# Second block's inner norms by token tile: pooling projection and the up projections' first two chunks begin with tile 0

## What is computed

```python
def second_block(x, ...):
    for layer in range(DEPTH):                       # DEPTH = 2
        j = layer // 2
        if layer % 2 == 0:
            y = even_mixer(x, ...)                   # mLSTM beside forgetting attention
        else:
            y = odd_mixer(x, ...)                    # state-space heads beside a pooling branch
        x = layer_norm(ALPHA * x + y, ln1_g[layer], ln1_b[layer])
        f = conv_ffn(x, ffn_w_up[layer], ffn_conv_w[layer], ffn_conv_b[layer], ffn_w_down[layer])
        x = layer_norm(ALPHA * x + f, ln2_g[layer], ln2_b[layer])
    return x
```

## Time and profile before

| | us |
|---|---|
| median of 3 runs | 1237.4 (1235.99 to 1239.66) |
| the profiled execution | 1235.73 |
| its span | 1233.9 |
| TensorE's products busy | 1188.3 (96%) |
| TensorE's weight loads busy | 1063.8 (86%) |
| POOL busy | 940.8 (76%) |
| ACT busy | 676.7 (55%) |
| DVE busy | 586.9 (48%) |
| mean granted TensorE clock | 0.987 |

### The profile page before, as it was taken

One profiled execution on the slowest core, in us unless ns is written; L12 is line 12 of the kernel. 1 busy time (PEld: TensorE's weight loads), 2 busy tenths in 40 slices (PEclk: granted clock), 3 DMA queues, 4 the chain that ended last, 5 costly groups with the idle time before them and its releaser, 6 DMA issues.

```text
span 1233.9 us, 20217 instructions
## 1 busy us (share of the span) xinstructions
PE 1188.3 (96%) x7776; PEld 1063.8 (86%) x7776; DVE 586.9 (48%) x1075; ACT 676.7 (55%) x932; POOL 940.8 (76%) x746
## 2 busy tenths in 40 slices
PE   6999999999989999999989999999998998999997
PEld 6988988999878998999978787888887986888886
DVE  4754344001684254200552746777404656777702
ACT  5765555443765555444453456576537665666641
POOL 6855889898724879989785455899896874999894
PEclk9999999999999999999999998999999999999999
DMA  8843445455411445545553243565454541555551
GB/s 306 243 151 117 168 161 205 171 184 193 172 69 70 171 147 208 196 167 187 197 175 137 99 137 135 185 231 201 171 204 146 196 171 68 201 199 206 186 197 35
DMA packets 33276, 208.56 MB, mean 169 GB/s; under 512 B 3448, under 2 KB 7672, under 8 KB 8744
## 3 DMA queue, kind: packets, MB, share of 16 engines
q1 hardware_dynamic: 29728, 198.17, 45.4%
q10 hardware_dynamic: 3464, 9.19, 2.3%
HBM read 206.29 MB, written 1.59 MB: 168 GB/s over the span
## 4 chain that ended last, share of the span: by engine, by line
PE 43%; POOL 36%; issue 16%; DVE 2%; ACT 2%; DMA 0%; POOLq 0%; DVEq 0%; SPq 0%; ACTq 0%
POOL w_lo L2490 36%; PE bank L346 13%; PE bank L348 7%; PE bank L294 7%; PE bank L295 6%; PE bank L296 6%; ACT w_hi L1169 1%; DMA raw<-stream 0%; PE bank L708 0%; PE bank L697 0%; PE bank L409 0%; PE bank L680 0%; ACT arena L1621 0%; DVE stats L1776 0%; DVE xs L1695 0%
## 5 line engine op out<-in xcount | busy, mean ns | idle before, releaser
L2490 POOL TENSOR_TENSOR w_lo<-raw,w_hi 128x512 fp32r<-128x512 f32 x740 | 938.1, 1307 | 275.2 <-ACT w_hi L1169 274.9
L1169 ACT ACTIVATE w_hi<-raw 128x2048 fp32r<-128x2048 f32 x185 | 352.1, 1911 | 173.0 <-PE bank L296 124.0
L346 PE MATMUL bank<-xs,w_hi 128*128 128x512 f32 x1024 | 363.7, 400 | 0.8 <-DVE xs L1695 0.7
L348 PE MATMUL bank<-xs,w_lo 128*128 128x256 f32 x1024 | 288.7, 282 | 0.0
L346 PEld LDWEIGHTS bank<-xs,w_hi 128*128 128x128 f32 x1024 | 193.7, 189 | 48.1 <-DVE xs L1695 2.1
L294 PE MATMUL bank<-hT_hi,w_hi 128*128 128x256 f32 x680 | 194.9, 287 | 2.3 <-issue 1.9
L348 PEld LDWEIGHTS bank<-xs,w_lo 128*128 128x128 f32 x1024 | 195.5, 191 | 0.0
L296 PE MATMUL bank<-hT_hi,w_lo 128*128 128x256 f32 x680 | 192.6, 283 | 0.0
L294 PE MATMUL bank<-xs,w_hi 128*128 128x256 f32 x576 | 168.0, 292 | 2.8 <-DVE xs L1695 1.2
L295 PE MATMUL bank<-xs,w_hi 128*128 128x256 f32 x576 | 165.0, 286 | 0.0
L296 PE MATMUL bank<-xs,w_lo 128*128 128x256 f32 x576 | 164.8, 286 | 0.0
(11 more groups left out here) (334 smaller groups left out, 1550.6 us busy)
## 6 DMA issues: line engine op xcount, KB each, us to landing
raw<-stream SPq DMA_DIRECT2D x185, 1024.0 KB, 4.9
arena<-ln_rows ACTq DMA_DIRECT2D x5, 1024.0 KB, 6.3
arena<-vec_scratch ACTq DMA_DIRECT2D x8, 256.0 KB, 6.1
con<-consts SPq DMA_DIRECT2D x1, 1288.0 KB
h<-x SPq DMA_DIRECT2D x2, 512.0 KB, 7.3
out<-h SPq DMA_DIRECT2D x4, 256.0 KB, 2.3
con<-pool_mat ACTq DMA_DIRECT2D x1, 768.0 KB, 9.8
vec_scratch<-vec_row ACTq DMA_DIRECT2D x1, 512.0 KB
```

Of the source, the lines that this page charges most:

```text
L346: mm(o[j][:, :], hi[:, k, s], xs[:, k, :, :].rearrange("p a t -> p (a t)"), start=(k == tiles_in[0]), stop=False, skip_group_check=True)
L348: last = mm(o[j][:, 0:T], lo[:, k, s], xs_hi[:, k, :], start=False, stop=(k == tiles_in[-1]), skip_group_check=True)
L1169: af(w_hi[:, c % CUT].rearrange("p a b -> p (a b)"), raw[:, c % RAW, :], ACT.Copy)\
L2490: ins = nc.gpsimd.tensor_tensor(w_lo[:, slot_c].rearrange("p a b -> p (a b)")[:, part], raw[:, slot_r, part], w_hi[:, slot_c].rearrange("p ...
```

## The change

At the norms 5, 6 and 7 the high and low halves are made by token tile: eight `high(n, t)` on ACT and eight `low_of(n, t)` on DVE in place of four each; `XS` counts eight for these norms.

- fup0 and fup1: a new `beside_by_tile` does the first two chunks together. It multiplies tile 0 with the high weights of both chunks pair by pair, then tile 1 with the high weights, and all low-weight products beside tile 1's. Its banks are fixed by `SHARED`, and the transposes of pairs 2 and 3 reuse the banks of pairs 0 and 1. The first transposes of tile 0 stand before and behind the last three products of the piece ahead. `dense_beside` goes on with chunk 2.
- Norm 6: DVE normalizes tile 0 in ACT's place; its transposes stand between the last products of fdown0; one cut moves ahead of ACT's part of the norm.
- od_pool moves ahead of dt in the stream and in the programs (`tile_by_tile`: tile 0 whole, then tile 1), ACT's copies of it too. The cb products move behind the pooled means, and ACT's copies of these means ahead of the first decay weights.
- At the mLSTM's second scores one bank is skipped (`turn[0] += 1`), which shifts the rotation behind it by one.

```diff
           ("gates", 1), ("ev_mv", 2), ("ev_qk", 4), ("ev_mo", 2), ("ev_fv", 2), ("ev_fqk", 4), ("ev_out", 4), ("fup0", 22), ("fdown0", 11),
-          ("dt", 1), ("od_xbc", 4), ("od_pool", 2), ("od_z", 2), ("od_out", 4), ("fup1", 22), ("fdown1", 11)]
+          ("od_pool", 2), ("dt", 1), ("od_xbc", 4), ("od_z", 2), ("od_out", 4), ("fup1", 22), ("fdown1", 11)]
...
         for name, k in [("n0", 4), ("ab", 8), ("n1", 4), ("n2", 4), ("cq", 2), ("c", 8), ("n3", 4), ("n4", 4),
-                        ("ml", 2), ("fx", 4), ("n5", 4), ("n6", 4), ("pool", 2), ("ssm", 4), ("n7", 4)]:
+                        ("ml", 2), ("fx", 4), ("n5", 8), ("n6", 8), ("pool", 2), ("ssm", 4), ("n7", 8)]:
...
                     after(i)
-            def dense_beside(name, rows, first=0, wait=None, tiles_in=tuple(range(8)), turn=None):
+            def beside_by_tile(name, i):
+                o, weights = {}, [chunk(START[name] + n) for n in range(2)]
+                for n in range(2):
+                    for j in range(2):
+                        key = (name, n, "second") if j else (name, n)
+                        o[n, j] = claim_bank(pe, key, SHARED[i][2 + j] if n else 6 + j)
+                turn[0] = 8 + SHARED[i][4]
+                def products(n, pair, t, low):
+                    hi, lo = weights[n]
+                    for k in (2 * pair, 2 * pair + 1):
+                        for j in range(2):
+                            s = slice(j * P, (j + 1) * P)
+                            z = o[n, j][:, :].rearrange("p (a t) -> p a t", a=2)[:, :, t * P:(t + 1) * P]
+                            last = mm(z, hi[:, k, s], xs[:, k, :, t * P:(t + 1) * P], start=(k == 0 and t == 0), stop=False,
+                                      skip_group_check=True)
+                            if low:
+                                last = mm(o[n, j][:, 0:T], lo[:, k, s], xs_hi[:, k, :], start=False, stop=(k == 7),
+                                          skip_group_check=True)
+                    return last
+                for pair in range(4):
+                    pe.wait_ge(S("xs_ready"), XS[f"n{i}"] - 7 + pair)
+                    if pair >= 2:
+                        second_turned(i, pair - 2)
+                    for n in range(2):
+                        products(n, pair, 0, False)
+                    if pair < 2:
+                        first_turned(i, 2 + pair)
+                for pairs in ((0, 1), (2, 3)):
+                    for n in range(2):
+                        for pair in pairs:
+                            if n == 0:
+                                pe.wait_ge(S("xs_ready"), XS[f"n{i}"] - 3 + pair)
+                            last = products(n, pair, 1, True)
+                            if n == 0 and pair < 2:
+                                second_turned(i, 2 + pair)
+                        if pairs == (2, 3):
+                            used_up(last)
+                for n in range(2):
+                    filled_by_chunk((name, n), START[name] + n)
+                    filled_by_chunk((name, n, "second"), START[name] + n)
+            def dense_beside(name, rows, first=0, wait=None, tiles_in=tuple(range(8))):
                 for i in range(first, rows):
...
                     for k in range(4):
                         last = by_tokens(o2, hi2, lo2, k, src, k, t, start=(k == 0), stop=(k == 3))
+                        if t == 1 and k == 2:
+                            first_turned(i, 0)
                     if t == 0:
...
                 filled_by_chunk((name, 1, 3), c + 1)
-                turned(i)
+                first_turned(i, 1)
...
+            def first_turned(i, n):
+                if i in SHARED and n >= 2:
+                    made[("turn", i, n)] = list(made[("turn", i, n - 2)])
+                    pe.wait_ge(S("xs_ready"), XS[f"n{i}"] - 9 + n)
+                elif i in SHARED:
+                    claim_bank(pe, ("turn", i, n), SHARED[i][n])
+                else:
...
+                if n == 3:
+                    evacuated(pe, last_piece(i, 1, 0))
+                else:
+                    pe.wait_ge(S("normed"), 3 * (i - 5) + n + 1)
+                transposed(i, n, 0).then_inc(S("first_turned"), 1)
             def second_turned(i, n):
-                pe.wait_ge(S("affine_act"), 4 * (i - 5) + n + 1)
+                if i in SHARED:
+                    pe.wait_ge(S("xs_ready"), XS[f"n{i}"] - 5 + n)
+                else:
+                    pe.wait_ge(S("xs_ready"), XS[f"n{i}"] - 7 + n)
                 if n == 3:
                     evacuated(pe, last_piece(i, 1, 1))
                 else:
                     pe.wait_ge(S("finished_dve"), 3 * (i - 5) + n + 1)
                 filled(transposed(i, n, 1), ("turn", i, n))
...
                         for u in range(4):
                             last = step(c, hi, lo, u, t)
+                            if t == 1 and c == chunks - 1 and i == 6:
+                                first_turned(i, u)
                         if t == 1:
...
-                    turned(i)
+            def tile_by_tile(name, i):
+                halves = [tuple(half_views(START[name] + kb)) for kb in range(2)]
+                for t in range(TT):
+                    o = claim(pe, (name, 0, t))
+                    for n in range(4):
+                        pe.wait_ge(S("xs_ready"), XS[f"n{i}"] - 7 + 4 * t + n)
+                        for k in (2 * n, 2 * n + 1):
+                            hi, lo = halves[k // 4]
+                            last = by_tokens(o, hi, lo, k % 4, (xs_hi, xs_lo), k, t, start=(k == 0), stop=(k == 7))
+                            if t == 1 and k % 4 == 3:
+                                used_up(last)
+                        if t == 0 and n >= 2:
+                            second_turned(i, n - 2)
+                        if t == 1 and n < 2:
+                            second_turned(i, n + 2)
+                    if t == 0:
+                        filled(last, (name, 0, 0))
...
+                if i == 0:
+                    turn[0] += 1
                 scores(2 + i)
...
             keep_gate_banks("fup0")
-            dense_beside("fup0", 22, wait="n5", turn=5)
+            dense_beside("fup0", 22, first=2)
             down_by_tokens("fdown0", 22, HT["fup0"], 6)
             rotating[0] = 8
-            dense("dt", 1, wait="n6", tiles=1, pairs=True, turn=6)
+            tile_by_tile("od_pool", 6)
+            dense("dt", 1, tiles=1)
             dense("od_xbc", 4)
...
-            token_major("od_pool", 1, None)
-            pe.wait_ge(S("xbc_ready"), 4)
-            for g in range(2):
-                o = claim(pe, ("cb", g))
-                mm(o[:, 0:T], xbc[:, 4 + g, 0:P], xbc[:, 6 + g, :], start=True, stop=True)
-                filled(mm(o[:, T:T + P], xbc[:, 4 + g, P:T], xbc[:, 6 + g, P:T], start=True, stop=True), ("cb", g))
...
                 filled(last, ("pooled", n))
+            pe.wait_ge(S("xbc_ready"), 4)
+            for g in range(2):
+                o = claim(pe, ("cb", g))
+                mm(o[:, 0:T], xbc[:, 4 + g, 0:P], xbc[:, 6 + g, :], start=True, stop=True)
+                filled(mm(o[:, T:T + P], xbc[:, 4 + g, P:T], xbc[:, 6 + g, P:T], start=True, stop=True), ("cb", g))
...
             last_half("od_out", 7, (xs_hi, xs_lo), "ssm", gated_sums)
+            beside_by_tile("fup1", 7)
             keep_gate_banks("fup1")
-            dense_beside("fup1", 22, wait="n7", turn=7)
+            dense_beside("fup1", 22, first=2)
...
+                            ins.then_inc(S("normed"), 1)
+                    def high(n, t):
+                        o = bank[made[("turn", i, n)][0]]
+                        s = slice(t * P, (t + 1) * P)
+                        af(xs_hi[:, 2 * n:2 * n + 2, s], o[:, :].rearrange("p (a b) -> p a b", a=2)[:, :, s], ACT.Copy)\
+                            .then_inc(S("xs_hi"), 1)
+                    def first_high(n):
+                        affine(n)
+                        act.wait_ge(S("affine_act"), 4 * (i - 5) + n + 1)
+                        high(n, 0)
+                    following = {5: "fup0", 6: "od_pool", 7: "fup1"}[i]
+                    deviate(0)
+                    if i == 6:
+                        cut(START[following] - 1 + AHEAD)
+                        first_high(0)
+                        first_high(1)
+                        first_high(2)
+                        deviate(1)
+                        first_high(3)
+                    else:
+                        act.wait_ge(S("inverted"), 2 * (i - 5) + 1)
+                        normalize(0)
+                        normalize(1)
+                        first_high(0)
+                        normalize(2)
+                        first_high(1)
+                        deviate(1)
+                        normalize(3)
+                        first_high(2)
+                        first_high(3)
+                    for n in range(4):
+                        full(act, ("turn", i, n))
```

(64 more changed lines are left out.)

90 lines of the change are left out of this document (52 added, 38 removed).

## The result

The changed kernel takes 1243.6 us in the median of 8 runs (1238.4 to 1248.6), the kernel before 1236.7; the ratio is 1.0058 with an interval of 1.0042 to 1.0075. Forecast was 1233.0 and a range up to 1238.5: the sign is wrong and the time lies outside. The profiled execution took 1242.65 (span 1240.9), against 1235.73 (1233.9), so the 7 us can be looked for in the two traces.

A forecast was written before the change was run, and what follows sets the result against it. The prediction took PE's work plus its waits and half clock at three inner norms as the bound. Gains of 3.1 (norm 5), 1.9 (norm 7) and 1.0 less 1.5 (norm 6) made 4.5 us: 1233.0, range 1229.5 to 1238.5.

The forecast's parts named there:

- norm 6, cb, od_z: Norm 6 onward: 1.0 us ahead after a new wait before cb, less 1.5 for half clock; net loss 0.5.
- Check (1): Norm 5: fup0's first product about 1.2 us behind the last piece's add, second chunk's end 15.9 behind, clock 1.00.
- Rival A: By-tile stretches at the norms: clock falls there too, each norm loses 1.4 us, total 1235.7; chance 0.18.
- Check (5): Up projections: products with split runs come 0.12 us apart; 0.16 or more fails the prediction.
- Rival C: Up projections at norms 5 and 7: split products are dearer; doubled, 1248.3 us, at half of that 1240.6; chance 0.09.
- Check (3): In front of cb: a PE wait of 4 us, released by ACT's SiLU, with granted clock 0.50 after it.
- Rival B: In front of cb: the wait leaves the clock alone or is shorter, 1231.4 down to 1229.5 us; chance 0.15.
- Check (2): Norm 6: PE busy from od_pool's second pair to dt's end, about 16.7 us behind fdown0's last product.
- counting the claims: Banks: the mLSTM skip leaves banks with long-emptied last users; costed at nothing, up to 0.5 us if one comes short.
- Check (4): Chunk 9 of both up projections: no PE wait on POOL, with less than a microsecond spare.
- after the change it comes about 0.2 to 0.5 later: fup0 chunk 9's low half: 0.2 to 0.5 us later, wanted 3.1 earlier, leaving 0 to 0.3 spare.
- Rival D: Norms and cb: pairs or fup's ninth chunk come late; gains of 1.0 to 1.5 lost at cb, 1237 us; chance 0.08.

The follow-up runs named there:

- experiment 1: Kernel before with only one bank skipped ahead of the mLSTM's third scores: ratio 0.9979 to the kernel before, median 1235.4 us.
- experiment 4: Changed kernel with the pooling projection's tile 1 written to long-free bank 7 instead of the next in turn: ratio 1.0045 to the kernel before.
- experiment 7: Changed kernel with norm 6's part and the order behind it put back, fourth chunk's cut not moved: ratio 1.0018 to the kernel before.
- experiment 2: Changed kernel with ACT's cut of the fourth chunk moved ahead of the wait for the gate banks: ratio 0.9998 to the kernel before, median 1237.1 us.
- experiment 6: Changed kernel with norm 6's part put back and the fourth chunk's cut ahead of the gate-bank wait: ratio 0.9943 to the kernel before, median 1230.7 us.
- experiment 8: Changed kernel with some 0.5 us of idle DVE work ahead of the rows' multiply in both up projections: ratio 1.0049 to the kernel before.
- experiment 5: Changed kernel with early fourth cut, rows' steps at the thirteenth gating step, pooling tile 1 in bank 7: ratio 0.9977 to the kernel before, median 1233.2 us.
- experiment 9: Changed kernel with early fourth cut, plus some 0.5 us of idle DVE work ahead of the rows' multiply: ratio 0.9987 to the kernel before.

## Why the prediction was wrong, point by point

The terms, forecast and as the two traces have them (differences of the table above):

| term | forecast | traces |
|---|---|---|
| bank left out in the mLSTM | 0 | -3.65 |
| norm 5 | -3.1 | -3.8 |
| given back in fup0 | 0 | +5.9 |
| norm 6, cb, od_z | +0.5 | +4.0 |
| norm 7 | -1.9 | -2.0 |
| given back in fup1 | 0 | +5.1 |
| fdown1 and the end | 0 | +1.5 |
| sum | -4.5 | +7.0 |

The row of norm 5 counts from the last add, which PE's transposes hold up: it comes 0.40 later than with the bank alone (740.60 against 740.20 in experiment 1). Counted as the forecast was, norm 5's part is 3.4.

**Norms 5 and 7: right.** Check (1): fup0's first product comes 1.30 us behind the start of the last piece's add (741.90 against 740.60; forecast 1.2), chunk 1 ends 15.7 behind it (forecast 15.9), clock 1.00 throughout, as in fup1's pair. In all nine traces with these products the clock is 1.00 over both pairs. Rival A falls.

**Split products: right.** Check (5): eight of them take this long, the last one's own length included:

```profile
741.90 1.19 PE L346 MATMUL bank<-xs,w_hi 128*128 128x256 f32 x8 [1.19 <-DVE xs L1796]
```

In tile 1's part they follow each other at 0.12. Rival C gave 1248.3 and the result lies toward it, but not for its reason. The rule of the Trainium skill (PSUM — Partial Sum Buffer, Specifications (TRN2)) that non-contiguous patterns slow matmuls does not show for two runs of 128 columns: 0.12 us each, as for one run of 256.

**The wait in front of cb: right.** Check (3): 4.36 us, forecast 4.4, released by ACT, and the clock 0.50 behind it:

```profile
988.90:992.00 3.10, 3.10 (x15) 3.02 (x15) 1.68 (x4) 1.80 (x4) 0.00 (x0) 0.50 1.00 391
```

(columns: PE, weight loads, DVE, ACT, POOL, then the clock). The first od_z chunk takes 7.1 us where it took 5.9; 1.5 was forecast for the clock, 1.2 of it show there. Rival B falls.

**dt's end: wrong by 3.1 us.** Check (2) wanted it 16.7 us behind fdown0's last product; it is 18.6. The true miss is larger, because that product itself now has transposes ahead of it: forecast was 953.3, or 951.8 with fdown0 1.54 earlier, and dt ends at 954.9. The step that failed is "counting the claims": I looked at the claims around norm 5 and not at the pooling projection's tile 1, whose bank held norm 6's last piece until DVE's fourth finished pair. The PE wait of 1.98 is that (experiment 4):

```profile
945.93 0.50 PE L294 MATMUL bank<-w_hi,xs 128*128 128x512 f32 x1 [1.98 <-DVE h L1967]
```

The other 1.1 are small idles and the transposes between the products. The chain from dt's end to the last SiLU is 32.4 to 33.1 us in all eleven traces (32.7 in the changed kernel, forecast 32.4), so every microsecond in front of dt goes to the end. That closes the account: 0.5 forecast, 3.1 for dt's end and 0.3 for the chain make 3.9 of the 4.0 in the traces. In the medians norm 6's part cost 5.0 (the changed kernel against experiment 7) and 6.8 (experiment 2 against 6). The idea behind it could be read from the prediction's own numbers: the pooling projection was cover behind the start of the xbc chain, and was moved ahead of that start.

**Chunk 9: wrong, and this decided.** Check (4) allowed no wait; there are 0.90, 1.20 and 2.05 at the chunks 3, 8 and 9 of fup0, and 0.91, 0.65 and 2.14 in fup1. The failing step is "after the change it comes about 0.2 to 0.5 later". It took the duration of the rows' steps (4.5) and the start of the cuts from the trace of before and moved them along. Two things moved otherwise. The banks of the first chunk had become those for which ACT waits ahead of its first cut in `gated`; a wait that had cost nothing when these banks were free early. And a gapless POOL holds DVE's multiply, 3.0 us a time. Given 0 to 0.3 us of spare, 3.0 had to become a PE wait. The spare itself was counted rightly: with the cut early, in experiment 2, there is no wait. I had checked chunk 2 and chunk 9, and not chunk 3, the first whose cut stands behind that wait. Rival D named "fup's ninth chunk comes late" but took the gains for 1.0 to 1.5, lost again at cb, and ended at 1237.

**The bank in the mLSTM: wrong, the other way.** The claims had been listed by hand, and the list showed that the third scores moved off the bank of the output gate; the wait for it stood in the trace of before, an idle of 2.73 us with 6.37 at half clock behind it. I used them as a price for other idles and did not ask whether the change removed them.

**The clock behind an idle: not as taken.** I let an idle of 1.94 us leave the clock at 1.00 and those of 2.18 and more lower it. The later traces don't keep to that. The idle at 372 us, 1.93 to 1.95 in all eleven, is followed by 1.00 in the kernel before, the changed one and experiments 4 and 6, and by 0.50 in the other seven. In experiment 1:

```profile
372.51:380.00 7.49, 7.49 (x51) 0.77 0.00 0
```

That is 51 products where the earlier trace rows has 64, and costs 1.5 us. And of the eight waits of 2.0 to 2.1 at chunk 9 (changed kernel, experiments 4, 7 and 8, both up projections) only two were followed by 0.50. The wait in front of cb, 4.0 to 4.8, has 0.50 behind it in all seven traces where it stands. So idles of 1.9 to 2.1 go either way from one trace to the next, and two traces can differ by 1.5 us and more by that alone.

**On DVE and POOL** the Trainium skill has a rule I had not weighed (SBUF — State Buffer, Who interferes with whom): a DVE instruction with two SBUF inputs contends with a GpSimd instruction that reads SBUF, and the one that comes second is blocked until the first ends. The kernel before agrees: multiply and split alternate, 2.29 us and 2.27 a piece, where such a DVE step alone takes 1.23 and a piece 1.29. The changed kernel goes beyond it: the multiply is held through five POOL pieces, not one. There the measurement decides. The same shows at norm 6, where the earlier cut put POOL beside the norm: DVE's first step on a pair took 1.38 at 938.59, and 0.48 in norm 5.

## What to carry to other kernels

Before work is moved ahead of a weight stream, list every wait that stands in front of the next cuts in program order, with the resource it waits for, and ask of each whether the change has changed that resource's last user. Treat a step's duration as belonging to its neighbours: a DVE step on two SBUF operands that takes 2.3 us between POOL's gaps took 6.3 when POOL had none, and a spare under that difference is no spare. And filler work is worth something only behind the start of the chain that it covers: moved ahead of it, it lengthens the path by itself and leaves a hole behind.

## What the runs showed of the hardware that was not expected

A DVE `tensor_tensor` on two SBUF operands was held for as long as POOL's split pieces followed each other without a gap at a chunk's end (up to 5 pieces, 6.29 us for 1.23 alone), and took turns with POOL, piece by piece, where POOL had had a gap of 0.2 to 0.6 us at the chunk's start. A shift of 0.5 us in phase changed neither. Why the gap matters, and not the piece, no run here shows.

The up projections' products run at two paces under a granted clock of 1.00. Windows of the same 50 us length, both full of fup products: the kernel before in fup0, then in fup1, then experiment 6 in fup1.

```profile
805.00:855.00 50.00, 50.00 (x285) 1.00 0.61 218
1110.00:1160.00 50.00, 50.00 (x291) 1.00 0.57 200
```
```profile
1110.00:1160.00 50.00, 50.00 (x285) 1.00 0.59 209
```

That is 285 or 291 instructions, 5.65 or 5.55 us a chunk, 2% apart. The pace can change within one execution. Of the eleven traces seven have both paces, and four (experiments 2, 5, 6 and 9, the kernels with the early cut) keep 5.65 in all of both up projections; with one trace for each kernel, whether the kernel or the execution sets the pace is not shown. The down projections have one pace in every trace, 0.227 us for 512 columns. Over the 44 chunks of the two up projections 2% are up to 4.7 us, as much as the effects studied here, and the cause stays open. Two traces can therefore be compared by their waits and by shifts over short stretches, but small differences of the whole need medians.
